# A two-layer hybrid backbone on one core: TensorE's rarely used passes moved to the end of its program, part of a projection moved forward, and the normaliser state as one more column

## What is computed

```python
for l in range(2):
    mod = silu(c) @ w_mod[l] + b_mod[l]            # shift, scale, gate of both sub-layers, 12 blocks of 512
    h = x * (1 + scale1) + shift1
    parts = h @ w_in[l] + b_in[l]                  # 1024 -> 18 chunks of 512, and 16 gate columns
    # mLSTM: the final state of the context group, both directions d
    #   C_new[d, h] = sum_s kw[s] v[s]^T ; n_new[d, h] = sum_s kw[s] ; m_new[d, h]
    # neighbourhood attention and HGRN2 on other chunks
    x = layer_norm(alpha * x + gate1 * (merged @ w_out[l]))
    x = layer_norm(alpha * x + gate2 * moe(x * (1 + scale2) + shift2))   # 16 experts, top 2 of one group of 4
```

## Time and profile before

| | us |
|---|---|
| median of 3 runs | 1324.93 |
| lowest and highest | 1323.29, 1327.27 |
| the profiled execution | 1326.44 |
| its span | 1324.7 |

### The profile page before, as it was taken

How to read it: one execution, slowest core, us unless ns; L and a number is a source line. 1 busy time by engine, 2 the same in 40 slices (tenths; PEclk the granted TensorE clock), 3 DMA queues, 4 the chain that set the end, 5 groups by cost and what they waited for, 6 DMA issues and landing times.

```text
span 1324.7 us, 19018 instructions
## 1 busy us (share of the span) xinstructions
PE 1278.5 (97%) x7508; PEld 780.2 (59%) x7508; DVE 631.8 (48%) x1227; ACT 267.9 (20%) x566; POOL 138.1 (10%) x115
## 2 busy tenths in 40 slices
PE   6999999999999999999989999999999999999995
PEld 2675577467744655555537655955884465555552
DVE  1224455476433664454452344555752356454445
ACT  0021121233301221111120212213430122111111
POOL 0002332023200000000000043301130000000000
PEclk9999999999999999999999999999999999999998
DMA  9854653666649999999993535355346589999991
GB/s 378 301 215 178 261 204 143 252 239 263 236 155 380 366 427 427 429 429 428 427 381 127 214 135 170 125 187 187 143 140 239 204 316 418 426 430 428 428 428 66
DMA packets 46892, 375.30 MB, mean 283 GB/s; under 512 B 15210, under 2 KB 19434, under 8 KB 23788
## 3 DMA queue, kind: packets, MB, share of 16 engines
q1 hardware_dynamic: 38400, 371.14, 69.6%
q10 hardware_dynamic: 8428, 3.29, 1.0%
HBM read 370.07 MB, written 4.33 MB: 283 GB/s over the span
## 4 chain that ended last, share of the span: by engine, by line
PE 87%; DVE 6%; DMA 5%; issue 1%; ACT 1%; DVEq 0%; SPq 0%
PE psum L1231 17%; PE psum L1371 13%; PE psum L1227 11%; PE psum L1181 9%; PE psum L1431 7%; PE psum L1256 6%; PE psum L1270 4%; DMA ring<-in_stream 4%; PE psum L949 3%; PE psum L1379 3%; PE psum L1003 2%; PE psum L1341 2%; PE psum L932 1%; DMA tbuf<-in_stream 1%; DVE tbuf L2312 1%
## 5 line engine op out<-in xcount | busy, mean ns | idle before, releaser
L1231 PE MATMUL psum<-ring,hT 128*128 128x512 f32 x512 | 230.6, 598 | 4.1 <-ACT hT L1518 2.2
L1231 PEld LDWEIGHTS psum<-ring,hT 128*128 128x128 f32 x512 | 94.3, 191 | 108.6 <-issue 103.2
L1227 PE MATMUL psum<-hT,ring 128*128 128x256 f32 x640 | 143.1, 380 | 0.0
L1227 PEld LDWEIGHTS psum<-hT,ring 128*128 128x128 f32 x640 | 120.1, 190 | 18.1 <-issue 3.1
L1371 PE MATMUL psum<-ch,tbuf 128*64 128x256 f32 x1024 | 113.3, 379 | 0.0
L1371 PE MATMUL psum<-ring,tbuf 128*64 128x256 f32 x960 | 106.8, 379 | 1.3 <-DMA ring<-in_stream 1.3
L1371 PEld LDWEIGHTS psum<-ch,tbuf 128*64 128x64 f32 x1024 | 73.4, 137 | 42.8 <-issue 8.0
L1371 PEld LDWEIGHTS psum<-ring,tbuf 128*64 128x64 f32 x960 | 68.7, 137 | 43.5 <-issue 7.9
L1256 PE MATMUL psum<-ring,tbuf 128*128 128x512 f32 x192 | 82.7, 592 | 0.0
L2292 DVE TENSOR_SCALAR tbuf<-psum,tbuf 128x512 f32<-128x512 f32 x32 | 24.0, 751 | 103.9 <-PE psum L1431 103.8
L2486 POOL TENSOR_SCALAR ldata<-ldata 128x512 f32<-128x512 f32 x24 | 50.3, 2097 | 221.3 <-ACT ldata L1658 221.3
(11 more groups left out here) (346 smaller groups left out, 1612.5 us busy)
## 6 DMA issues: line engine op xcount, KB each, us to landing
ring<-in_stream SPq DMA_DIRECT2D x105, 2048.0 KB, 11.3
ch<-in_stream SPq DMA_DIRECT2D x51, 2048.0 KB, 17.9
bias_ring<-in_b_in SPq DMA_DIRECT2D x26, 256.0 KB, 8.2
ldata<-in_ldata SPq DMA_DIRECT2D x2, 2329.0 KB, 18.2
tbuf<-in_stream SPq DMA_DIRECT2D x2, 2048.0 KB, 14.5
ring<-in_stream SPq DMA_DIRECT2D x4, 1024.0 KB, 13.6
hbuf<-in_ln SPq DMA_DIRECT2D x4, 1024.0 KB, 9.1
ldata<-in_stream SPq DMA_DIRECT2D x2, 2048.0 KB, 13.4
```

The lines of the kernel that those rows point to most:

```text
L1227: mm = pe.matmul(psum[:, PJ + g, part * G * P:(part + 1) * G * P], w[:, k, (2 * g + part) * P:(2 * g + part + 1) * P], hT[:, k, :], start= ...
L1231: mm = pe.matmul(bank(PJ + g), hT[:, k, g * P:(g + 1) * P], w[:, k, :], start=(k == 0), stop=(k == KT - 1))
```

## The change

1. PE's body for further passes of both layers stands behind both layers. Behind the experts stands a conditional branch whose usual side is the code that follows; only the rare case jumps. At the end of the two layers an unconditional jump leads around both bodies. The other engines keep their If and Else.
2. In layer 0, chunk 1 is loaded in two halves, the first before the two early modulation slots and the second where chunk 1 was loaded. PE computes the first half of its contraction (k = 0..3, four blocks of `second_chunk_half`) around `early_mod(1)`: two blocks ahead of the modulation products, one between them and their columns, one behind the columns. These sums stand in PSUM banks 2 and 4. Quarters 4 to 7 then add k = 4..7 only.
3. The round state is split by direction: 4 products of [128 x 129] at quarter 29 and 4 at quarter 31, whose 129th column (ones in `values`) gives n. The round norm_state goes; a round norm_turn at quarter 33 turns the eight columns of n by one product with the identity. C is stored by two DMAs of half the size, n as eight rows. All other rounds keep their quarters.

```diff
@@ -147,7 +147,7 @@
-    T_ROUNDS += [("state", 0, 0), ("norm_state", 0, 0)] if _g == 0 else [("inter", 1, 0)]
+    T_ROUNDS += [("state", 0, 0), ("state", 0, 1), ("norm_turn", 0, 0)] if _g == 0 else [("inter", 1, 0)]
...
@@ -367,6 +368,7 @@
+        PROJ_BANK = {(0, 1): (EX, PP)}
...
@@ -769,9 +773,16 @@
                 sp.dma_start(ring[:, j, 0:SLOT // 2], source[:, 0:SLOT // 2]).then_inc(first_half_loaded, 16)
                 if l == 0:
+                    sp.wait_ge(slot_used, BASE[l] + (i + 2))
+                    sp.dma_start(ring[:, (i + 1) % RING, 0:SLOT // 2], dram["stream"][stream_slot("in", l, 1), :, 0:SLOT // 2]).then_inc(next_half_loaded, 16)
                     load_early(2)
                     load_early(3)
                 sp.dma_start(ring[:, j, SLOT // 2:SLOT], source[:, SLOT // 2:SLOT]).then_inc(slot_loaded[j], 16)
+
+            def second_chunk_end(i):
+
+                j = i % RING
+                sp.dma_start(ring[:, j, SLOT // 2:SLOT], dram["stream"][stream_slot("in", 0, 1), :, SLOT // 2:SLOT]).then_inc(slot_loaded[j], 16)
...
@@ -962,9 +976,18 @@
                 mm.then_inc(early_filled, 1)
-                pe.wait_ge(ident_loaded, 16)
+
+            def early_columns(part):
+
                 pe.wait_ge(rows_added, part + 1)
                 mod_columns([0], T + 1).then_inc(cols_filled, 1)
+
+            def second_chunk_half(block):
+
+                w = ring[:, AT[0]["in", 0, 1] % RING, :].rearrange("p (k n) -> p k n", k=KT)
+                for k in range(KT // 2):
+                    pe.matmul(psum[:, PROJ_BANK[0, 1][block // 2], (block % 2) * G * P:(block % 2 + 1) * G * P], w[:, k, block * P:(block + 1) * P],
+                              hT[:, k, :], start=(k == 0 and block % 2 == 0), stop=False, skip_group_check=True)
...
@@ -1065,12 +1088,11 @@
                     if kind == "state":
-                        for d in range(2):
-                            for h, hp in enumerate(tiles):
-                                mm = pe.matmul(psum[:, T + d, hp], dg[:, d, hp], values[:, 0, h, 0:P], start=True, stop=True)
-                    if kind == "norm_state":
-                        for d in range(2):
-                            mm = pe.matmul(psum[0:1, T + d, :], c_("ones"), dg[:, d, :], start=True, stop=True)
+                        for h, hp in enumerate(tiles):
+                            mm = pe.matmul(psum[:, T + h // 2, (h % 2) * (P + 1):(h % 2 + 1) * (P + 1)], dg[:, i, hp], values[:, 0, h, :],
+                                           start=True, stop=True)
+                    if kind == "norm_turn":
+                        mm = pe.matmul(psum[0:2 * HEADS, T, 0:P], n_col.rearrange("p d h -> p (d h)"), ident, start=True, stop=True)
...
@@ -1139,7 +1163,13 @@
                             if g == 0:
+                                pe.wait_ge(next_half_loaded, 16)
+                                second_chunk_half(0)
+                                second_chunk_half(1)
                                 early_mod(1)
+                                second_chunk_half(2)
+                                early_columns(1)
+                                second_chunk_half(3)
                             pe.wait_ge(*((xt_first, 1) if g else (xt_read_act, 2)))
...
@@ -1223,9 +1253,10 @@
                     if c in BY_FEATURE:
-                        for k in range(KT):
+                        b, half_done = PROJ_BANK.get((l, c), (PJ, PJ + 1))[g], (l, c) in PROJ_BANK
+                        for k in range(KT // 2 if half_done else 0, KT):
...
@@ -1454,6 +1484,21 @@
+                n_fullest = experts()
+                left_at[l] = nc.cur_bb
+                pe.br_cond(n_fullest > CAP, f"pe_further_{l}", f"pe_one_pass_{l}")
+                nc.switch_bb(f"pe_one_pass_{l}")
+                pe.sem_inc(x_pe, PE_FURTHER * FURTHER)
+                pe.br(f"pe_passes_done_{l}")
+                nc.switch_bb(f"pe_passes_done_{l}", parent=left_at[l])
+                if l + 1 < DEPTH:
+                    for j in range(len(LAYER_MODS)):
+                        mm = layer_mod(j)
+                    mm.then_inc(layer_mods_filled, 1)
+            pe.br("pe_layers_done")
...
@@ -1494,11 +1539,13 @@
-                further_passes(pe, l, experts(), further_expert, lambda: None, sums_read, [(x_pe, PE_FURTHER * FURTHER)])
...
+                with nc.body(f"pe_further_{l}", parent=left_at[l], valid_engines=[mybir.EngineType.PE]):
...
@@ -1593,17 +1640,18 @@
                     elif kind == "state":
...
+                        sums = psum[:, T:T + 2, 0:2 * (P + 1)].rearrange("p b (h n) -> p b h n", h=2)
+                        act.activation(n_col[:, i, :].rearrange("p (b h) -> p b h", b=2), sums[:, :, :, P], ACT.Copy)
+                        act.activation(em[:, i, :].rearrange("p (b h n) -> p b h n", b=2, h=2), sums[:, :, :, 0:P], ACT.Copy).then_inc(t_act, 1)
+                        act.wait_ge(t_act, l * NT + (n + 1))
+                        act.dma_start(out["C"][l, i].rearrange("h k e -> k h e"), heads(em[:, i, :])).then_inc(state_stored, 16)
+                    elif kind == "norm_turn":
+                        turned_n = tbuf[0:2 * HEADS, 4 * W:4 * W + P]
+                        act.activation(turned_n, psum[0:2 * HEADS, T, 0:P], ACT.Copy).then_inc(t_act, 1)
+                        act.wait_ge(t_act, l * NT + (n + 1))
+                        act.dma_start(out["n"][l].rearrange("a (r k) -> (a r) k", r=2 * HEADS), turned_n).then_inc(state_stored, 16)
```

More of the change, by code:

```diff
@@ L162, in ready_quarter @@
     return 4 * chunk + (4 if chunk in BY_FEATURE else 2 * g + 2)
-SPARE = {"prep": 1, ("read_f", 0): 1, "silu": 1, "state": 1, "norm_state": 2, "cumsum": 1, "max": 1, ("gate", 0): 1, ("decay", 1): 1, "na_scores": 1, ("na_probs", 1): 1}
+SPARE = {"prep": 1, ("read_f", 0): 1, "silu": 1, "state": 1, "cumsum": 1, "max": 1, ("gate", 0): 1, ("decay", 1): 1, "na_scores": 1, ("na_probs", 1): 1}
 ROTATE_AT = 29
@@ L349, in build @@
         h4b = small(4)
+        n_col = small(2, 4)
         n_mx = small(4)
@@ L452, in build @@
         first_half_loaded = sem("first_half_loaded")
+        next_half_loaded = sem("next_half_loaded")
         bias_loaded = [sem(f"bias_loaded{i}") for i in range(RING)]
@@ L535, in build @@
         y_stored = sem("y_stored")
-        N_STATE = 4 * 16
+        N_STATE = 5 * 16
         class Chain:
@@ L658, in build @@
         PE_FURTHER, ACT_FURTHER, DVE_FURTHER = 5, 3, 15
+        halves_of = [slice(0, CAP), slice(CAP, P)]
         def further(per, l, p, e, done):
@@ L701, in t_works @@
             if eng == "act":
-                return kind in ("gates", "forget", "decay", "turn", "state", "norm_state", "gate", "na_back", "na_cache", "na_scores", "na_probs")
-            return kind not in ("gates", "state", "norm_state", "na_back", "na_cache")
+                return kind in ("gates", "forget", "decay", "turn", "state", "norm_turn", "gate", "na_back", "na_cache", "na_scores", "na_probs")
+            return kind not in ("gates", "state", "norm_turn", "na_back", "na_cache")
         def worked(works, rounds, eng, n):
@@ L788, in _ @@
                         first_chunk(l, i)
+                    elif (kind, c, l) == ("in", 1, 0):
+                        second_chunk_end(i)
                     else:
@@ L920, in _ @@
             pe.wait_ge(silu_c, 1)
+            left_at = {}
             def slot(l, *item):
@@ L1107, in _ @@
                     early_mod(0)
+                    pe.wait_ge(ident_loaded, 16)
+                    early_columns(0)
                     pe.wait_ge(x_loaded, 16)
@@ L1224, in _ @@
                     if c in BY_FEATURE:
-                        for k in range(KT):
-                            mm = pe.matmul(psum[:, PJ + g, part * G * P:(part + 1) * G * P], w[:, k, (2 * g + part) * P:(2 * g + part + 1) * P],
-                                           hT[:, k, :], start=(k == 0), stop=(k == KT - 1))
+                        b, half_done = PROJ_BANK.get((l, c), (PJ, PJ + 1))[g], (l, c) in PROJ_BANK
+                        for k in range(KT // 2 if half_done else 0, KT):
+                            mm = pe.matmul(psum[:, b, part * G * P:(part + 1) * G * P], w[:, k, (2 * g + part) * P:(2 * g + part + 1) * P],
+                                           hT[:, k, :], start=(k == 0), stop=(k == KT - 1), skip_group_check=half_done)
                     else:
@@ L1329, in _ @@
                 w_down_last = last_down.rearrange("p (k n) -> p k n", k=BT)
-                halves_of = [slice(0, CAP), slice(CAP, P)]
                 def gather_split(n, part, at, first=False):
@@ L1456, in experts @@
                     return n_fullest
+                n_fullest = experts()
[10 more added lines that the diff above has]
+            pe.br("pe_layers_done")
+            for l in range(DEPTH):
                 def further_expert(p, e):
@@ L1495, in sums_read @@
                     pe.wait_ge(x_dve, (l + 1) * FURTHER * DVE_FURTHER + 1)
```

(11 more changed lines are left out.)

2 lines of the change are left out of this document (1 added, 1 removed).

## The result

The changed kernel takes 1316.95 us (median of 6 runs, 1314.02 to 1320.17) against 1326.1 for the kernel before in the same comparison (6 runs, 1323.29 to 1329.44): ratio 0.9927, 95% interval 0.9913 to 0.9942, so that the gain of 9.15 us is clear of noise. Its profiled execution took 1318.85 us, with a span of 1317.1, against 1326.44 and 1324.7. The forecast was 1315.5, in a range of 1312.2 to 1321.

What follows compares the result with a forecast made beforehand. TensorE, busy in 97% of the span, was taken as the bound. Gains of 3.0 (start of layer 0), 4.8 (end of layer 0) and 3.1 (final state), 10.9 us, took 1326.44 to 1315.5; range 1312.2 to 1321.

Steps and rivals of the forecast that it cites:

- Start of layer 0: Half of chunk 1 fills TensorE's holes: 3.0 us gained, from 3.1 holes and 1.7 clock less waits 0.5 and 1.25.
- rival (c): Start of layer 0: second modulation slot lands late, TensorE waits and the clock falls; 1319.2 us, chance 0.09.
- the slow clock hangs on the holes: Start of layer 0: clock of 0.79 follows 3.1 us of holes, so 1.7 us more goes with them.
- End of layer 0: Contiguous code removes the instruction-fetch hole in layer_mod and the slow clock behind it: 4.8 us gained.
- Rival (b): End of layer 0: instruction fetch still stalls TensorE in the new layout, no gain there; 1320.3 us, chance 0.11.
- (d): Layer 1: shifted expert-loop code overfills instruction memory, each of six turns refetches, 3.3 us each; 1335 us, chance 0.04.
- The split of the gain: End of layer 0: a 3.31 us hole on issue, plus 1.55 us for the slow clock after it.
- The prediction's aside on rival (d): Expert loop: no queue 8 packet from 506 to 655, said to disagree with an instruction memory of two blocks.
- Final state: Both layers: dropping round norm_state, adding norm_turn of 0.24 us, gains 1.57 us per layer, 3.1 in all; moved stores free.
- the landing has 3 us before ACT is even at its gate... Cost nothing: State stores issued at quarter 33, done about 181, ACT's gate at 184.30; TensorE late only beyond some 5 us.
- The prediction's own sign of being wrong: Among the listed signs: a wait of TensorE for ACT's gate at quarter 36.
- The third slow stretch: Slow clock from 1083 to 1087, away from the change; 1.7 us that may come or go by run, left in.

Runs made afterwards that it cites:

- after_warm_short: Kernel with both edits plus 4 and 3 idle TensorE products around the first modulation slot's landing: 1313.38 us, ratio 0.9906 to the kernel before.
- part 1 alone: Kernel before with only TensorE's bodies for further passes moved behind both layers: 1321.31 us, ratio 0.9966.
- part 3 alone: Kernel before with only the state split by direction and n as a 129th column: 1324.95 us, ratio 0.9988.
- short jump: Kernel before with TensorE's body for further passes cut to one semaphore increment, the jump kept: 1321.8 us, ratio 0.9968.
- before_filled: Kernel before with 3 and 9 idle products in the two TensorE holes at the start of layer 0: 1326.24 us, ratio 1.000.
- after_gate: Changed kernel with turned n in kTa and ACT waiting for the state stores before its gate's last instruction: 1318.05 us, ratio 0.9936 to the kernel before.
- both edits: Changed kernel with the edits of after_gate and after_cumsum: 1314.94 us, 0.9913 to the kernel before; in a later comparison 1313.63 us, 0.9909.
- after_cumsum: Changed kernel with one spare quarter behind the round forget, so context cumsum, max and decay stand one quarter later: 1315.9 us, 0.9926 to the kernel before.
- part 2 alone: Kernel before with only half of chunk 1 moved forward in layer 0: 1323.53 us, ratio 0.9975.

## Why the prediction held, and where it did not

- **Start of layer 0: right.** 3.15 us for 3.0. Remaining wait for hT 0.38 for 0.5, wait at cumsum 1.16 for 1.25, no wait on the early slots, so rival (c) did not come; not even in after_warm_short, where their products began as early as 31.69. That the slow clock hangs on the holes was argued then and is shown now: the granted clock from 38 to 46 us is 0.79, 0.71, 0.86 and 0.65 in the four profiles of kernels with the holes open (before, part 1 alone, part 3 alone, short jump), and 1.00 in before_filled and in all nine with part 2.
- **End of layer 0: right.** 4.78 us for 4.8. Rival (b), another stall at a block's edge, did not come, nor did (d). The split of the gain is less sure than I wrote. The hole of 3 to 4 us was there in every kernel with the long jump, but the slow clock behind it was not: one of the four profiles, part 3 alone, shows the hole without it. Timeline of TensorE there:

```profile
676.80 4.50 PE L950 MATMUL psum<-ch,scZ 128*32 128x512 f32 x40 [3.03 <-issue]
```

  Forty instructions in 4.50, 0.11 each, are at 2.4 GHz. From `layer_mod` to the transposes of g = 1 this kernel took 687.97 - 672.71 = 15.3 us, against 17.3 before and 12.5 after: without the slow stretch the gain would be 2.8 us. Whether the other 2.0 hang on the execution or on where the hole falls, one profile of each kernel does not say; the measured gains of part 1 alone (4.5) and of the short jump (0.0032, 4.2) are nearer to the full 4.8.
  The prediction's aside on rival (d), that the rows disagree with a memory of two blocks, is not shown. The window of the earlier trace rows holds 1282 products and 1280 weight loads in 5.4 turns of 27.8 us, 477 shown instructions a turn, and no row says how many fill a block. What stands is that no packet of queue q8 moved there.
- **Final state: the removal right, the move wrong.** 1.4 us in layer 0 and 1.5 in layer 1 for 1.57: norm_turn took 0.31 from its start to the next product, not 0.24. The step that failed is "the landing has 3 us before ACT is even at its gate... Cost nothing", and with it "only beyond some 5 us is TensorE" late. Timeline of all engines in the changed kernel (ACTq are ScalarE's DMA issues):

```profile
177.70 0.27 ACTq L1654 DMA_DIRECT2D out_m<-sm  x1
...
183.69 0.63 ACT L1660 ACTIVATE tbuf<-ch 128x512 f32<-128x512 f32 x1 [1.99 <-DMA out_m<-sm]
...
184.43 0.43 DVE L2028 TENSOR_SCALAR tbuf<-tbuf 128x512 f32<-128x512 f32 x1 [2.90 <-ACT tbuf L1660]
...
186.22 1.49 DVE L2030 TENSOR_TENSOR ch<-tbuf 128x512 f32<-128x512 f32 x1 [1.36 <-ACT tbuf L1663]
...
187.63 1.52 DVE L400 TENSOR_TENSOR hbuf<-hbuf 128x512 f32<-128x512 f32 x1
...
189.25 0.68 ACT L1594 ACTIVATE hbuf<-hbuf 128x512 f32<-128x512 f32 x1 [3.06 <-DVE hbuf L400]
...
189.99 1.23 PE L1026 MATMUL psum<-hbuf 128*128 128x128 f32 x8 [0.95 <-ACT hbuf L1594]
```

  The last store was issued at 177.70 and ACT could have begun its gate at about 181.7; its release came at 183.69, 6.0 us after the issue, and I had no row for a small store's landing. The prediction's own sign of being wrong, a wait of TensorE at quarter 36, is what appeared. Worse, I asked only when TensorE next looks at this gate. The work of the other mixer stands in the same queues: behind the late gate DVE's L400, behind that ACT's L1594, and for that TensorE waits at the next level, with 2 us of delay on ACT enough for it. after_gate took the wait away. In layer 1 ACT's gate ran without a wait. Timeline of ScalarE:

```profile
822.59 0.27 ACTq L1654 DMA_DIRECT2D out_m<-sm  x1
825.57 0.86 ACT L1594 ACTIVATE hbuf<-hbuf 128x512 f32<-128x512 f32 x1 [3.86 <-PE psum L1026]
826.33 0.61 ACT L1660 ACTIVATE tbuf<-ch 128x512 f32<-128x512 f32 x1
```

  Here the store had landed within 3.7 us. A load was under way in both layers. In layer 0 SP had issued a ring slot at 170.47, a bias in small pieces at 170.85 and a slot at 172.36, and their bytes moved until about 183.0; in layer 1 it had issued one slot at 817.25, whose bytes moved until about 825.0. The last packets of the stores (queue q10) moved between 182.75 and 183.00, and between 825.00 and 825.25: each time as the load ran out. In the kernel before, the three stores went out in a gap between loads (last issue at 172.89), and their last packet had moved by 174.25. That the loads hold the stores up fits all this, but no run here moved a load to try it.
- **The sum.** Forecast 10.9 us against 1326.44. The stages of the two profiles give 3.15 + 1.41 - 1.20 - 0.05 + 4.78 + 1.38 = 9.5, and the later rise of the clock in the second execution takes 1.9 of it: 7.6. The medians differ by 9.15. Of the 1.4 us short of the forecast the stores' 1.2 is the main part. That 1315.5 came so close to the median of 1316.95 is in part luck: the forecast started from one execution, 1326.44, which turned out near the median of six (1326.1) and not 1.5 above it.
- **The third slow stretch stayed.** It lies in the experts of layer 1, away from the change, and the prediction left it in. It is in 8 of the 14 profiles here, two of them of the changed kernel, and costs 1.6 us where it comes. Timeline of TensorE, the same 32 products in the changed kernel and in the second profile with both edits:

```profile
1074.49 5.44 PE L1381 MATMUL psum<-tbuf,ch 128*128 128x128 f32 x32 [0.90 <-DVE tbuf L2321]
1070.51 3.81 PE L1381 MATMUL psum<-tbuf,ch 128*128 128x128 f32 x32 [0.90 <-DVE tbuf L2320]
```

## What to carry to other kernels

A wait of some 3 us that ends on nothing, in a run of products just behind a jump, was code being fetched here: look for a packet of an instruction queue inside it, and put a body that is hardly ever run behind everything else, or make it short. When a store or a load is moved towards a wait, take its landing from a row under the traffic of that place, and follow each queue behind the waiting instruction through all the streams of work that share it, not only through its own. Work that fills a hole gives back the hole and, where it holds the clock, more; price the clock's share apart from it, since at some places it comes and goes from profile to profile.

## What the runs showed of the hardware

- The clock in the first 26 us differs from profile to profile. The second early slot's 16 instructions took 1.92 us in one profile (part 3 alone) and 3.64 in others of the same start, and quarter 0's products began between 20.80 (part 3 alone) and 25.23 us (after_cumsum) for it, in kernels whose work up to there is alike. In some the clock was up and fell back: in after_both the granted clock was 0.50 from 16 to 26 us. The kernel with both edits began quarter 0 at 23.96 in one profile and at 22.70 in the other, so the execution decides at least part of it; both profiles of the changed kernel were late (24.64 and 25.00), and whether the change has a share in that is not shown. The 4.4 us between the extremes are as much as the runs of one kernel spread (2.6 to 7.2 us), but only the profiled run of each shows its clock. Products that do nothing from 4.28 us on brought it up by 9.5 in both profiles that had them.
- A jump over a long body cost 3.31, 3.17, 3.03 and 4.21 us in four kernels that differ by a few instructions (before, part 2 alone, part 3 alone, before_filled), and nothing over a body of one instruction. The hole came 0, 7 or 8 instructions into `layer_mod`. The expert loop's own jumps back left no such hole in any profile.
- A store of a few bytes took 6.0 us to release its waiter in one place and at most 3.7 in another of the same program, its last packet moving each time as the load under way ended.
